# A ten-stage transformer kernel: q, k and v as rows with a late row scale, attention products one step deep, low parts written over the raw weights

## The chip, the cores and the metric

The kernel runs on one core of one Trainium2 chip. The metric is the device time of one execution in microseconds (us), lower is better. Beside the time of each run there is one profiled execution with its own time and its span, from the first to the last instruction.

## The reference, cut to what matters

256 tokens of width 1024, float32, pass ten stages; each is `x = x + c * rms_norm(f(rms_norm(x)))`.

```python
# moba:  z = h @ w_in (1024 x 2560): gated unit, 8 heads of causal attention, causal convolution; @ w_out
# cross: q = h @ w_xq; k, v = split(m @ w_xkv); 4 heads of 256; @ w_xo     (m: normed memory, 256 rows)
# relu:  square(relu(h @ w_ff1)) @ w_ff2                                  (1024 x 4096 x 1024)
# glu0..glu3: (silu(h @ wg) * (h @ wu)) @ wd                              (width 2816)
# diff:  q, k, v = split(h @ w_in, 3)                                     (1024 x 3072)
    q = concatenate([_rotate(q[..., :16], ang), q[..., 16:]], -1)    # per 64 columns; k alike
#        8 heads: softmax(q1 k1) - lam * softmax(q2 k2), times v, then a norm of each head's 128 columns
# near:  q, k, v = split(h @ w_in, 3); 16 heads of 64 with a relative bias inside a window; @ w_out
def rms_norm(x, g):
    return x * rsqrt(mean(x * x, -1) + EPS) * g
```

The order is moba, cross, relu, glu0, diff, glu1, glu2, near, glu3.

## The kernel before, in words

**Chunks.** All weights pass as 226 chunks of 1 MB, each 128 partitions x 2048 float32. SyncE loads a chunk into one of three `raw` buffers (`load`, L373); ScalarE casts it to a rounded high part (`w_hi<-raw`, L555); VectorE subtracts to get the low part (`w_lo<-raw,w_hi`, L772). A product takes three matmuls for each tile: high x high, high x low, low x high. Cast and subtraction of one chunk are the word `s` of the plan (or `h` and `l` apart). Load c waits for `lo_done`: the subtraction of chunk c-3, which frees its raw buffer (L376). The high and low parts have three slots of their own, and a fourth that lies over `qT`/`kT` in the stages that do not hold them (`slots_of_chunks`). A cast waits until the chunk that held its slot has been used.

**The plan.** `PLAN` is a table of words for each stage; every engine walks the same words in order and does its part of each. `q1` is a chunk's product, `.0` and `.1` its halves (for in-rows products the two tiles of 128 tokens), `:0`/`:1` halves by tokens of a product that lies transposed. `post`, `gain`, `sq`, `turn` are steps of the norm between stages for token tile 0 or 1: scale and add the result, multiply the gain, squares, and the turn of the rows by TensorE to `hT`.

**Products.** `transposed` (L1086) holds a 128 x 128 weight tile and moves 256 tokens, giving q or k with heads on the partitions; `in_rows` (L1101) holds a token tile and moves up to 512 weight columns. Before, q and k are `transposed` in all four attention stages, and v of diff and near is `in_rows`. Cross has three q chunks in the `:` form, in which every weight tile is used twice with 128 tokens each. diff multiplies each q and k by a matrix (`rot`, L1244) and mixes with cosines and sines over 128 x 512 elements (L1036, L1038, L1040).

**The row scale.** The norm's 1/root is put in at the turn for the attention stages: `diagonal` (L795) makes a diagonal matrix from it, which waits for squares (ScalarE) and root (GpSimd), and the turn is a matmul with that (L1127, 16 half steps). For the FFN stages the turn is a transpose by the identity (L1125, 8), and the scale comes in at the activation (`LATE_SCALE`, L73).

**Attention steps.** In step s, TensorE makes the scores of unit s (S, L1146 or L1141), turns the probabilities of unit s-1 (P, L1157) and weighs the values of unit s-2 (W, L1172 or L1185). A half or a whole chunk stands between two steps. VectorE finds the maximum (M, L961) and normalises (N, L969 to L981), ScalarE takes the exponential (E, L618) and copies the turned probabilities (Q, L628). diff adds a norm for each unit: squares (A, ScalarE L647), a root (GpSimd L517, L518), the scaling (B, VectorE L991), a turn (Z, TensorE L1193), and the copy and subtraction of the result (O, L607 and L1010). These letters are used below.

Of the kernel before, what the change touches and what calls it, by code (L numbers as in the profile page):

```python
# [14 lines left out]
P = 128  # L15
# [5 lines left out]
NRAW = 3  # L21
# [11 lines left out]

HEAD_GLU = ("ga0.0 post1 s gb0.0 gain1 s ua0.0 turn1 sq1 ub0.0 G0.0 H0.0 ga0.1 s gb0.1 G0.1 s ua0.1 s "
# [5 lines left out]
             "ub1.1 G1.0 H1.0 G1.1 H1.1 s da0 s db0 s ")  # L40
# [3 lines left out]
HEAD_V = "va0.0 post1 s vb0.0 gain1 sq1 s vc0.0 turn1 vd0.0 va0.1 "  # L44
PLAN = {
# [22 lines left out]
CHUNK_NAMES = {"moba": "g a u w K V q k v o", "cross": "q o", "relu": "ua ub da db",  # L68
               "diff": "va vb vc vd q k o", "near": "va vb vc vd q k o"}
GLU_NAMES = "ga gb ua ub da db g u d"  # L70
N_NORMS = len(STAGES)

LATE_SCALE = {i + 1 for i, kind in enumerate(STAGES) if kind in FFN}  # L73

Word = namedtuple("Word", "name digit form half c n first done step_next at")


def read_plans():

    plans, chunks, c_next = {}, [], 0  # L80
    for at, kind in enumerate(STAGES):
        names = CHUNK_NAMES.get(kind, GLU_NAMES).split()
        seen, n_next, words = {}, 0, []
        for text in PLAN[kind].split():
            form = ":" if ":" in text else "." if "." in text else ""
            text, half = (text[:-2], int(text[-1])) if form else (text, None)
            name = text.rstrip("0123456789")
# [11 lines left out]
            words.append(Word(name, digit, form, half, c, n, first, done, False, at))
        real = [i for i, w in enumerate(words) if w.name not in "shl"]  # L100
        for i, after in zip(real, real[1:]):
            words[i] = words[i]._replace(step_next=words[after].name == "step")
        plans[kind] = words
# [10 lines left out]
def slots_of_chunks():  # L114


    held, slots, before = [-1] * 4, [], []
    for c, (kind, name, _) in enumerate(CHUNKS):
        free = range(4) if kind in FFN or name in ("va", "vb", "vc", "vd") else range(3)
        slot = min(free, key=lambda s: held[s])  # L120
        slots.append(slot)
        before.append(held[slot])
        held[slot] = c
    return slots, before


SLOT, BEFORE = slots_of_chunks()


ATT = {  # L130
    "moba": dict(units=8, u0=0, e0=0, per_out=2, scale=0.125, parts=1, per_chunk=4),
    "cross": dict(units=4, u0=8, e0=4, per_out=1, scale=1.0 / 16, parts=1, per_chunk=1),
    "diff": dict(units=8, u0=12, e0=8, per_out=1, scale=0.125, parts=2, per_chunk=2),
    "near": dict(units=16, u0=20, e0=16, per_out=2, scale=0.125, parts=1, per_chunk=4),
}
# [11 lines left out]
def products_of(kind, s):

    a = ATT[kind]
    number = {(w.name, w.digit): w.n for w in WORDS[kind] if w.c is not None}  # L150
    heads = []
    if s < a["units"]:
        heads += [(letter, s // a["per_chunk"]) for letter in "qk"]
    if s >= 2:
        heads.append(("v", (s - 2) // a["per_chunk"]))
    return N0[kind] + 1 + max(number.get(head, 0) for head in heads)


ROT_ORDER = [w.digit for w in WORDS["diff"] if w.name == "rot"]
# [6 lines left out]
def shape_tables():  # L166
# [9 lines left out]
    mean = np.full((P, P), 1 / P, np.float32)  # L176
    rot = np.zeros((P, P), np.float32)
    inv = np.float32(500000.0) ** (-np.arange(0, 16, 2, dtype=np.float32) / np.float32(16))
    ang = (t.astype(np.float32)[:, None] * inv[None, :].astype(np.float32)).astype(np.float32)
# [1252 lines left out]
```

## Time and profile before

| | us |
|---|---|
| median of 3 runs | 1533.74 (1533.03 to 1534.62) |
| profiled execution, its time | 1531.81 |
| its span | 1530.1 |

| engine | busy, share of the span |
|---|---|
| TensorE matmul (PE) | 95% |
| TensorE weight load (PEld) | 80% |
| VectorE (DVE) | 56% |
| ScalarE (ACT) | 45% |
| GpSimd (POOL) | 9% |

The profile lists for each engine its busy time, the waits and what ended them, and the chain that ended last. A matmul's own duration overlaps its neighbour's, so the pace of TensorE is read from starts or from counts in a window.

### The profile page before, as it was taken

What the parts mean: (1) busy time and instruction counts of PE and PEld (TensorE: products, weight loads), DVE (VectorE), ACT (ScalarE), POOL (GpSimd) and SP (SyncE); (2) the same over time, 40 slices, a digit from 0 to 9 for tenths busy, and PEclk for the clock granted to TensorE, in tenths of its full rate; (3) what the DMA queues carried; (4) which work ended last, traced back from release to release, by engine and by line L of the source; (5) the groups of instructions that cost most, each with busy time, mean ns of one, the idle gap of its engine ahead of it and who ended that gap; (6) DMA issues with size and microseconds to landing.
All of it is one profiled execution on the core that took longest, in us unless ns stands there. A gap on an engine that the chain in (4) does not pass through costs nothing.

```text
span 1530.1 us, 18751 instructions
## 1 busy us (share of the span) xinstructions
PE 1454.7 (95%) x7753; PEld 1231.5 (80%) x7753; DVE 851.8 (56%) x910; ACT 689.2 (45%) x886; POOL 139.7 (9%) x248
## 2 busy tenths in 40 slices
PE   6999899999999999998679999999999899999996
PEld 6998798788888888887558888888888777688885
DVE  4976635555475445646656454655446565655443
ACT  4546435444445444444345444444334444454441
POOL 1000100101101110000011111011100600000000
PEclk9999999999999999999899999999999999999998
DMA  8754233656547655452226555476554623265550
GB/s 273 242 168 136 91 121 120 233 190 198 190 159 240 195 189 188 150 173 83 83 83 225 192 195 192 153 239 196 190 195 138 202 73 108 90 228 192 192 165 28
DMA packets 133664, 256.28 MB, mean 167 GB/s; under 512 B 6280, under 2 KB 57164, under 8 KB 133580
## 3 DMA queue, kind: packets, MB, share of 16 engines
q1 hardware_dynamic: 129484, 251.94, 49.9%
q0 software_dynamic: 4096, 3.15, 0.7%
q8 instruction: 61, 1.00, 0.3%
q14 instruction: 23, 0.19, 0.0%
HBM read 254.02 MB, written 1.05 MB: 167 GB/s over the span
## 4 chain that ended last, share of the span: by engine, by line
PE 89%; DVE 3%; ACT 3%; issue 2%; DMA 1%; POOL 1%; SPq 1%; DVEq 0%; POOLq 0%; ACTq 0%
PE ps L1108 23%; PE ps L1110 23%; PE ps L1109 23%; PE ps L1094 4%; PE ps L1096 4%; PE ps L1095 4%; PE ps L1146 2%; PE ps L1185 2%; PE ps L1334 2%; PE ps L1157 1%; DVE w_lo L772 1%; ACT w_hi L555 1%; ACT t L618 1%; DMA raw<-w_in 1%; PE ps L1125 1%
## 5 line engine op out<-in xcount | busy, mean ns | idle before, releaser
L772 DVE TENSOR_TENSOR w_lo<-raw,w_hi 128x2048 fp32r<-128x2048 f32 x226 | 519.4, 2300 | 446.3 <-ACT w_hi L555 446.0
L555 ACT CAST w_hi<-raw 128x2048 fp32r<-128x2048 f32 x226 | 431.1, 1910 | 398.8 <-PE ps L1110 368.0
L1108 PE MATMUL ps<-w_hi,hT_hi 128*128 128x512 f32 (+1 forms) x1008 | 377.7, 375 | 1.9 <-DVE w_lo L772 1.6
L1110 PE MATMUL ps<-w_hi,hT_lo 128*128 128x512 f32 (+1 forms) x1008 | 374.0, 371 | 0.0
L1109 PE MATMUL ps<-w_lo,hT_hi 128*128 128x512 f32 (+1 forms) x1008 | 373.6, 371 | 0.0
L1108 PE MATMUL ps<-w_hi,yT_hi 128*128 128x512 f32 (+1 forms) x672 | 261.5, 389 | 14.4 <-DVE rope_t L1036 7.5
L1109 PE MATMUL ps<-w_lo,yT_hi 128*128 128x512 f32 (+1 forms) x672 | 257.8, 384 | 0.0
L1110 PE MATMUL ps<-w_hi,yT_lo 128*128 128x512 f32 (+1 forms) x672 | 257.4, 383 | 0.0
L1108 PEld LDWEIGHTS ps<-w_hi,hT_hi 128*128 128x128 f32 x1008 | 189.9, 188 | 37.4 <-DVE w_lo L772 5.2
L1110 PEld LDWEIGHTS ps<-w_hi,hT_lo 128*128 128x128 f32 x1008 | 189.9, 188 | 32.9
L1109 PEld LDWEIGHTS ps<-w_lo,hT_hi 128*128 128x128 f32 x1008 | 190.0, 189 | 31.6
L1108 PEld LDWEIGHTS ps<-w_hi,yT_hi 128*128 128x128 f32 x672 | 128.3, 191 | 43.2 <-DVE w_lo L772 14.8
L1110 PEld LDWEIGHTS ps<-w_hi,yT_lo 128*128 128x128 f32 x672 | 128.1, 191 | 24.9
L1109 PEld LDWEIGHTS ps<-w_lo,yT_hi 128*128 128x128 f32 x672 | 128.1, 191 | 23.2
L1094 PE MATMUL ps<-hT_hi,w_hi 128*128 128x256 f32 (+1 forms) x480 | 140.7, 293 | 4.1 <-DVE hT_lo L801 2.7
L1095 PE MATMUL ps<-hT_lo,w_hi 128*128 128x256 f32 (+1 forms) x480 | 136.0, 283 | 0.0
L1096 PE MATMUL ps<-hT_hi,w_lo 128*128 128x256 f32 (+1 forms) x480 | 135.8, 283 | 0.0
L475 POOL DMA_DIRECT2D big<-na_rpb x128 | 66.2, 519 | 498.6 <-PE ps L1110 498.3
L1094 PEld LDWEIGHTS ps<-hT_hi,w_hi 128*128 128x128 f32 x480 | 93.1, 194 | 10.2 <-issue 8.2
L1095 PEld LDWEIGHTS ps<-hT_lo,w_hi 128*128 128x128 f32 x480 | 93.1, 194 | 0.8 <-issue 0.5
L1096 PEld LDWEIGHTS ps<-hT_hi,w_lo 128*128 128x128 f32 x480 | 93.0, 194 | 0.0
L487 POOL TENSOR_SCALAR rstd<-ssq 128x1 f32<-128x1 f32 x38 | 14.7, 388 | 714.8 <-ACT probT L561 696.3
(151 smaller groups left out, 1138.7 us busy)
## 6 DMA issues: line engine op xcount, KB each, us to landing
raw<-ffn_wg SPq DMA_DIRECT2D x44, 1024.0 KB, 5.3
raw<-ffn_wu SPq DMA_DIRECT2D x44, 1024.0 KB, 5.3
raw<-ffn_wd SPq DMA_DIRECT2D x44, 1024.0 KB, 5.3
raw<-w_ff SPq DMA_DIRECT2D x32, 1024.0 KB, 5.6
raw<-diff_w_in SPq DMA_DIRECT2D x12, 1024.0 KB, 5.1
raw<-na_w_in SPq DMA_DIRECT2D x12, 1024.0 KB, 5.1
raw<-w_in SPq DMA_DIRECT2D x10, 1024.0 KB, 5.6
raw<-w_xkv SPq DMA_DIRECT2D x8, 1024.0 KB, 5.8
```

The source lines that it names most:

```text
L475: pool.dma_start(bias[p:p + 1], bass.AP(rpb.tensor, (5 - r) * 31 + 15 - c, [[465, 16], [31, 6], [1, 64]])).then_inc(bias_in, 16)
L555: act.copy(hi_part(c), raw[:, c % NRAW, :]).then_inc(hi_done, 1)
L772: dve.tensor_tensor(lo_part(c), raw[:, c % NRAW, :], hi_part(c), ALU.subtract).then_inc(lo_done, 1)
L1094: pe.matmul(o, hi, src[0][:, k, tokens], start=(k == 0), stop=False)
L1095: pe.matmul(o, hi, src[1][:, k, tokens], start=False, stop=False)
L1096: ins = pe.matmul(o, lo, src[0][:, k, tokens], start=False, stop=(k == KT - 1))
L1108: pe.matmul(o, hi, wh[:, i, cols], start=first and i == 0, stop=False)
L1109: pe.matmul(o, hi, wl[:, i, cols], start=False, stop=False)
L1110: ins = pe.matmul(o, lo, wh[:, i, cols], start=False, stop=last and i == len(tiles) - 1)
L1146: ins = pe.matmul(o, qT[rows, head // 2, t * P:(t + 1) * P], kT[rows, head // 2, :], start=True, stop=True)
L1185: ins = pe.matmul(o, values[:, kt, cols], probT[:, b, 256 * kt:256 * kt + 256], start=(kt == 0), stop=(kt == TT - 1))
L1334: ins = pe.transpose(up_bank(kind, b, t)[:, cols], hraw[:, t, cols], ident)
```

## The change

1. q, k and v of cross, diff and near all come `in_rows`, as groups of 512 columns: chunks `qa qb` (two halves of the 1024 inner rows) are group q0, `qc qd` q1, and so on. ScalarE copies a group's rows out of PSUM times the row scale (`rq`, `rk`, `rv`); TensorE turns q and k (`tq`, `tk`); ScalarE copies the turned tile. The rotation of diff touches 16 of each 64 columns of the rows, four small VectorE operations for a tile.
2. The turn of the norm is a transpose for all stages but the first; no diagonal matrix for cross, diff and near. `lambda` moves from diff to relu.
3. The steps are written by `attention`: S of unit s, then the step's chunks, then P of s-1 and W of s-2; a split follows one step after its chunk. moba, cross, diff and near use it.
4. `raw` has five buffers, and the low part is written over the raw chunk. There are four high slots, at all times. Load c waits for `chunk_used` of c-5.

```diff
-NRAW = 3
+NRAW = 5
+NHI = 4
+def attention(kind, units, fill, carry=0):
+    lags = 4 if kind == "diff" else 3
+    words = []
+    for s in range(units + lags - 1):
+        def unit(names, lag):
+            words.extend(f"{name}{s - lag}" for name in names if 0 <= s - lag < units)
+        if kind == "diff":
+            unit("B", 3)
+        unit("SM", 0)
+        if kind == "diff":
+            unit("ZO", 3)
+        unit("E", 0)
+        chunks = fill.get(s, "").split()
+        words += chunks
+        unit("N", 0)
+        words += ["s"] * carry
+        carry = sum(word[0] in "qkvo" and not word.endswith(".0") for word in chunks)
+        unit("PQ", 1)
+        unit("WA" if kind == "diff" else "WO", 2)
+    return " ".join(words + ["s"] * carry) + " "
-HEAD_V = "va0.0 post1 s vb0.0 gain1 sq1 s vc0.0 turn1 vd0.0 va0.1 "
+HEAD_QK = ("qa0.0 post1 s qb0.0 gain1 s ka0.0 turn1 rq0.0 kb0.0 tq0.0 sq1 rk0.0 qa0.1 s qb0.1 tk0.0 s rq0.1 ka0.1 s "
+           "tq0.1 kb0.1 s rk0.1 va0.0 tk0.1 ")
-    "cross": ("q0:0 post1 s gain1 sq1 q1:0 turn1 q2:0 q0:1 s q1:1 h 0 l q2:1 h 1 l q3.0 2 q3.1 h 3 l "
-              "o0.0 o0.1 s 4 s o1.0 5 o2.0 o3.0 post0 gain0 o1.1 s o2.1 turn0 sq0 o3.1"),
+    "cross": ("qa0.0 post1 s qb0.0 gain1 s qc0.0 turn1 rq0.0 sq1 qd0.0 tq0.0 qa0.1 s rq1.0 qb0.1 tq1.0 s rq0.1 qc0.1 "
+              "s tq0.1 " +
+              attention("cross", 4, {0: "qd0.1 rq1.1", 1: "tq1.1", 3: "o0.0", 4: "o0.1", 5: "o1.0"}) +
+              "o2.0 o3.0 post0 gain0 o1.1 s o2.1 turn0 sq0 o3.1"),
+    "diff": (HEAD_QK +
+             attention("diff", 8, {0: "va0.1 vb0 rv0", 1: "qc0 qd0.0", 2: "qd0.1 rq1 kc0", 3: "tq1 kd0 rk1 vc0.0 tk1",
+                                   4: "vc0.1", 5: "vd0.0", 6: "vd0.1 rv1", 7: "o0.0", 8: "o0.1", 9: "o1.0",
+                                   10: "o2.0 o1.1"}) +
+             "o3.0 post0 gain0 o2.1 turn0 sq0 o3.1"),
...
+        w_lo = nc.alloc_sbuf_tensor_at("w_lo", [P, NRAW, CH], F32R, offset=nc.sbuf_base - 4 * NRAW * CH)
+        w_hi = sb("w_hi", [P, NHI, CH], F32R)
...
                 if c >= NRAW:
-                    sp.wait_ge(lo_done, c - NRAW + 1)
+                    sp.wait_ge(used, c - NRAW + 1)
...
-                if BEFORE[c] >= 0:
-                    act.wait_ge(used, BEFORE[c] + 1)
+                if c >= NHI:
+                    act.wait_ge(used, c - NHI + 1)
...
+            def rows_word(kind, word):
+                letter, nb = word.name[1], word.digit
+                g, count = group_at(kind, letter, nb)
+                for t in range(TT) if word.half is None else (word.half,):
+                    bank = group_bank(g, t)
+                    k = TT * (word.at + 1) + t
+                    if word.name[0] == "t":
+                        act.wait_ge(rows_turned[t], count)
+                        dst = qT if letter == "q" else kT
+                        act.copy(dst[:, 4 * nb:4 * nb + 4, t * P:(t + 1) * P],
+                                 bank.rearrange("p (k s) -> p k s", k=4)).then_inc(qk_evac[t], 1)
+                        continue
...
+                        act.activation(rows[:, t, :], bank, ACT.Copy, scale=rstd[:, k:k + 1]).then_inc(rows_out[t], 1)
```

**Where instructions move.** The unit's norm in diff, TensorE. A step of the kernel before, from the turn of unit s-3 to the next product:

```order
L1193 MATMUL ps<-tab,sub_out 128x128 [waits sub_on,b_evac]
L1193 MATMUL ps<-tab,sub_out 128x128
L1146 MATMUL ps<-kT,qT 128x256 [waits exp_ready,rope_done]
L1146 MATMUL ps<-kT,qT 128x256 x3
L1157 MATMUL ps<-tab,prob 128x128 [waits probT_ready,prob_ready]
L1157 MATMUL ps<-tab,prob 128x128 x3
L1172 MATMUL ps<-vv,probT 128x128 [waits out_lo,probT_ready]
L1172 MATMUL ps<-vv,probT 128x128 x3
L1094 MATMUL ps<-hT_hi,w_hi 128x256 [waits b_evac,lo_done]
```

The same place after the change, from the last turn of group k1 (reading `rows`) to the next product:

```order
L1308 MATMUL ps<-tab,rows 128x128 [waits rope_done_1]
L1308 MATMUL ps<-tab,rows 128x128 x3
L1160 MATMUL ps<-tab,prob 128x128 [waits probT_ready,prob_ready]
L1160 MATMUL ps<-tab,prob 128x128 x3
L1175 MATMUL ps<-vv,probT 128x128 [waits probT_ready,out_lo,v_evac_1,v_evac_0]
L1175 MATMUL ps<-vv,probT 128x128 x3
L1149 MATMUL ps<-kT,qT 128x256 [waits exp_ready,qk_evac_1,qk_evac_0]
L1149 MATMUL ps<-kT,qT 128x256 x3
L1196 MATMUL ps<-tab,sub_out 128x128 [waits sub_on]
L1196 MATMUL ps<-tab,sub_out 128x128
L1110 MATMUL ps<-w_hi,hT_hi 128x512 [waits qk_evac_1]
```

Before, a half chunk stood between W (`probT`,`vv`) and the turn Z (`sub_out`) of the same unit, and Z opened the step. Now S (`kT`,`qT`) alone stands between them, and the product comes behind Z.

ScalarE at the end of that same step (step 3 of diff) after the change; `rows<-ps,rstd` is the scaled copy of group k1, `kT<-ps` the copy of its turned tiles:

```order
L724 ACTIVATE rows<-ps,rstd 128x512 [waits rows_turned_0,r_pre,chunk_half_used]
L724 ACTIVATE rows<-ps,rstd 128x512 [waits rows_turned_1,r_pre,chunk_used]
L713 COPY kT<-ps 128x4x128 [waits rows_turned_0]
L713 COPY kT<-ps 128x4x128 [waits rows_turned_1]
L561 CAST w_hi<-raw 128x2048 [waits chunk_used,chunk_landed_1]
L561 CAST w_hi<-raw 128x2048 [waits chunk_used,chunk_landed_2]
L628 COPY probT<-ps 128x512 [waits out_ready,probT_turned]
L636 ACTIVATE att_bias,sub_stat<-ps 128x128 [waits sub_sq,out_ready]
```

Both casts of the step stand behind the copies of the turned tiles and ahead of Q (`probT<-ps`) and A (`sub_stat<-ps`), on which the next Z hangs. Before, the cast of a step stood behind A:

```order
L607 CAST yT_hi<-ps 128x256 [waits sub_turned]
L618 ACTIVATE t,denom<-ps,neg_top 128x256 [waits prob_ready,max_ready]
L618 ACTIVATE t,denom<-ps,neg_top 128x256 x3
L628 COPY probT<-ps 128x512 [waits out_ready,probT_turned]
L647 ACTIVATE att_bias,sub_stat<-ps 128x128 [waits sub_sq,sub_on,out_ready]
L647 ACTIVATE att_bias,sub_stat<-ps 128x128 [waits sub_sq]
L699 COPY kT<-ps 128x512 [waits chunk_used]
L555 CAST w_hi<-raw 128x2048 [waits chunk_used,chunk_landed_1]
```

ScalarE in the head of diff after the change, from the cast of its fifth chunk to the second copy of token tile 1:

```order
L561 CAST w_hi<-raw 128x2048 [waits chunk_used,chunk_landed_4]
L713 COPY kT<-ps 128x4x128 [waits rows_turned_0]
L561 CAST w_hi<-raw 128x2048 [waits chunk_used,chunk_landed_0]
L724 ACTIVATE rows<-ps,rstd 128x512 [waits rows_turned_1,r_pre,chunk_used]
L561 CAST w_hi<-raw 128x2048 [waits chunk_used,chunk_landed_1]
L713 COPY qT<-ps 128x4x128 [waits rows_turned_1]
L561 CAST w_hi<-raw 128x2048 [waits chunk_used,chunk_landed_2]
L724 ACTIVATE rows<-ps,rstd 128x512 [waits rows_turned_1,r_pre,chunk_used]
L713 COPY kT<-ps 128x4x128 [waits rows_turned_1]
```

The scaled copies of tile 1 (`rows_turned_1`) stand behind casts, each of which waits for a chunk to land.

## Rows read from the trace of the kernel before

**Rows 1.** The page: the chain that ended last, by engine.

```profile
PE 89%; DVE 3%; ACT 3%; issue 2%; DMA 1%; POOL 1%; SPq 1%; DVEq 0%; POOLq 0%; ACTq 0%
```

**Rows 2.** Windows: busy time, clock, DMA of stages cross, diff, near (columns: first line).

```profile
core 0: us, PE busy (x) PEld busy (x) DVE busy (x) ACT busy (x) POOL busy (x), PEclk, DMA share, GB/s
...
183.20:262.40 79.20, 78.39 (x537) 72.11 (x536) 37.55 (x49) 32.54 (x56) 4.96 (x8) 1.00 0.33 111
...
636.50:802.20 165.70, 134.57 (x810) 116.17 (x809) 96.33 (x152) 72.51 (x162) 12.71 (x24) 0.93 0.34 114
...
1178.50:1330.90 152.40, 141.78 (x794) 112.53 (x792) 89.27 (x154) 72.28 (x137) 26.81 (x24) 0.98 0.36 117
```

**Rows 3.** Windows inside three product runs; the first (x) counts matmuls.

```profile
183.20:193.80 10.60, 10.60 (x97) 10.58 (x95) 6.04 (x8) 3.88 (x7) 3.74 (x4) 1.00 0.41 151
...
310.90:321.70 10.80, 10.80 (x49) 8.97 (x48) 5.34 (x3) 4.40 (x3) 1.03 (x2) 1.00 0.54 192
...
1232.50:1235.50 3.00, 3.00 (x25) 2.92 (x24) 1.77 (x5) 1.57 (x5) 0.00 (x0) 1.00 0.00 0
```

**Rows 4.** Waits of PE, whole span: us in total, times, longest.

```profile
PE ps L1127 <- DVE rope_t L795: 13.6, 4, 10.3
...
PE ps L1108 <- DVE rope_t L1036: 7.5, 1, 7.5
...
PE ps L1146 <- issue: 5.8, 1, 5.8
```

**Rows 5.** Timeline of PE, two turns: start us, us, engine, line, out<-in.

```profile
193.88 2.00 PE L1127 MATMUL ps<-rope_t,t 128*128 128x128 f32 x16
...
810.70 1.03 PE L1125 MATMUL ps<-tab,t 128*128 128x128 f32 x8
```

**Rows 6.** Timeline of DVE at the end of moba.

```profile
174.49 1.28 DVE L786 TENSOR_TENSOR t<-x_rows,gain 128x512 f32<-128x512 f32 x2
...
176.62 0.28 DVE L795 TENSOR_SCALAR rope_t<-tab,rstd 128x128 f32<-128x128 f32 x1 [0.85 <-POOL rstd L488]
```

**Rows 7.** Timeline of PE, a turn Z of diff.

```profile
767.32 0.41 PE L1193 MATMUL ps<-tab,sub_out 128*128 128x128 f32 x2 [2.62 <-DVE sub_out L991]
```

**Rows 8.** Timeline, the norm of one unit of diff, from its product to its turn.

```profile
779.09 0.48 PE L1108 MATMUL ps<-w_hi,yT_hi 128*128 128x512 f32 x1
...
780.52 0.70 POOL L518 TENSOR_TENSOR sub_stat<-sub_stat,minus_half 128x2 f32<-128x2 f32 x1
...
782.01 0.41 PE L1193 MATMUL ps<-tab,sub_out 128*128 128x128 f32 x2
```

**Rows 9.** Timeline of DVE, unit 0 of diff: maximum, normalising, next split.

```profile
685.36 1.22 DVE L961 TENSOR_REDUCE top<-ps 128x4 f32<-128x1024 f32 x1
...
690.73 2.29 DVE L772 TENSOR_TENSOR w_lo<-raw,w_hi 128x2048 fp32r<-128x2048 f32 x1
```

**Rows 10.** Windows: clock after two idle times of PE.

```profile
704.50:709.50 5.00, 4.97 (x22) 4.24 (x23) 1.40 (x2) 1.39 (x7) 0.00 (x0) 0.50 0.46 186
...
767.30:771.30 4.00, 3.98 (x23) 3.47 (x23) 1.82 (x3) 1.35 (x6) 0.00 (x0) 0.68 0.02 4
```

**Rows 11.** Timeline, head of relu.

```profile
277.68 1.91 ACT L555 CAST w_hi<-raw 128x2048 fp32r<-128x2048 f32 x1 [3.06 <-PE ps L1110]
...
284.95 1.08 ACT L730 CAST yT_hi<-ps 128x512 fp32r<-128x512 f32 x2
...
288.12 0.47 PE L1108 MATMUL ps<-w_hi,yT_hi 128*128 128x512 f32 x1 [1.45 <-DVE yT_lo L1061]
```

**Rows 12.** Timeline of ACT, head of glu0.

```profile
462.89 1.91 ACT L555 CAST w_hi<-raw 128x2048 fp32r<-128x2048 f32 x1 [1.64 <-PE ps L1110]
...
477.52 1.91 ACT L555 CAST w_hi<-raw 128x2048 fp32r<-128x2048 f32 x1 [3.24 <-DMA raw<-ffn_wd]
```

**Rows 13.** DMA issues: count, KB each, median us to landing.

```profile
raw<-ffn_wg SPq DMA_DIRECT2D x44, 1024.0 KB, 5.3
```

**Rows 14.** Window: DMA while two loads were queued.

```profile
271.00:276.00 5.00, 5.00 (x28) 4.23 (x27) 2.59 (x4) 2.89 (x7) 0.86 (x2) 1.00 1.02 407
```

More of the change, by code:

```diff
@@ L67 @@
 FFN = ("relu", "glu0", "glu1", "glu2", "glu3")
-CHUNK_NAMES = {"moba": "g a u w K V q k v o", "cross": "q o", "relu": "ua ub da db",
-               "diff": "va vb vc vd q k o", "near": "va vb vc vd q k o"}
-GLU_NAMES = "ga gb ua ub da db g u d"
+IN_ROWS = [letter + part for letter in "qkv" for part in "abcd"]
+CHUNK_NAMES = {"moba": "g a u w K V q k v o".split(), "relu": "ua ub da db".split(),
+               "cross": IN_ROWS + ["o"], "diff": IN_ROWS + ["o"], "near": IN_ROWS + ["o"]}
+GLU_NAMES = "ga gb ua ub da db g u d".split()
 N_NORMS = len(STAGES)
-LATE_SCALE = {i + 1 for i, kind in enumerate(STAGES) if kind in FFN}
-Word = namedtuple("Word", "name digit form half c n first done step_next at")
+Word = namedtuple("Word", "name digit half c n first done at")
 def read_plans():
@@ L96, in read_plans @@
                     c_next += 1
-                    n_next += kind not in FFN and name != "o" and name[1:] == ""
+                    n_next += kind == "moba" and name != "o"
                 c, n = seen[name, digit]
[L99 to L102, printed above, removed]
+            words.append(Word(name, digit, half, c, n, first, done, at))
         plans[kind] = words
@@ L111 @@
 FIRST = [min(c for c, key in enumerate(CHUNKS) if key[0] == kind) for kind in STAGES]
[L114 to L127, printed above, removed]
 ATT = {
[L131 to L134, printed above, removed]
-}
@@ L147, in products_of @@
[L147 to L159, printed above, removed]
+GROUPS = {kind: [(w.name[0], "abcd".index(w.name[1]) // 2) for w in WORDS[kind] if w.first and w.name[1:] in ("a", "c")]
+          for kind in ("cross", "diff", "near")}
@@ L160, with number_of, group_at @@
+QK0 = {"cross": 0, "diff": 2, "near": 6}
+VV0 = {"diff": 0, "near": 2}
+def number_of(letter, digit):
+    return [w.n for w in WORDS["moba"] if (w.name, w.digit) == (letter, digit)][0]
+def group_at(kind, letter, nb):
+    g = GROUPS[kind].index((letter, nb))
+    same = [i for i, other in enumerate(GROUPS[kind][:g + 1]) if (other[0] == "v") == (letter == "v")]
+    return g, (VV0 if letter == "v" else QK0)[kind] + len(same)
 OUT_ORDER = {kind: [w.digit for w in WORDS[kind] if w.name == "o" and w.first] for kind in ATT}
@@ L513, in _ @@
                         pre_root(n, t)
[L514 to L515 removed]
+                    if kind == "diff" and word.name == "B":
+                        u = word.digit
                         pool.wait_ge(sub_sq_done, TT * (u + 1))
@@ L527, in _ @@
                                 load_bias(bias_rows[kind] + p)
-                    if kind == "near" and (word.name, word.digit, word.first) == ("q", 0, True):
+                    if kind == "near" and word.name == "rk" and (word.digit, word.half) == (0, 0):
                         pool.wait_ge(bias_in, 16 * P)
@@ L831, in norm_word @@
                     gain_rows(n, x, t)
-                if word.name == "sq" and n not in LATE_SCALE:
-                    diagonal(n, t)
                 if word.name == "turn":
@@ L1116, in turn @@
                     pe.wait_ge(h_lo, 4 * n + 2)
-                late = n in LATE_SCALE
-                if not late:
-                    pe.wait_ge(diag_set, len([m for m in range(n) if m not in LATE_SCALE]) * TT + t + 1)
+                if n < 2:
+                    pe.wait_ge(diag_set, TT * n + t + 1)
                 for b in range(2):
```

414 lines of the change are left out of this document (197 added, 217 removed), and 9 rows, old and new, of the table PLAN.

## The prediction

> **What bounds the kernel now.** I read the page first: TensorE is 89% of the chain that ended last [rows 1]. The reader should see that only TensorE's own work, its pace or its idle time can move the end. The windows by stage say where idle time is [rows 2]: cross lasts 79.2 us, diff 165.7, near 152.4, of which TensorE is idle for 0.8, 31.1 (165.7 less 134.57) and 10.6. The clock in diff is 0.93 on average, which loses 0.07 x 165.7 = 11.6 us more; in near 0.98, 3.0 us. The FFN stages have almost none of either. Third, the windows inside product runs give the pace [rows 3]: 48 matmuls of 512 columns in 10.8 us, 5.4 us a chunk; q or k with 256 columns, 25 in 3.0 us, 0.12 each, 5.76 us a chunk of 48; the `:` form of cross, 97 in 10.6 us, 0.109 each, and a chunk needs 96 of them, 10.5 us. Fourth, TensorE's waits [rows 4]: it waits for the diagonal matrix (13.6 us in four places), and in diff for the rotation (7.5, and the 5.8 put down to issue, which ends when the rotation of k1 ends).
>
> **The change, part by part.** The sum is made against the profiled execution, 1531.8 us.
>
> *Turns of the norm.* A turn by the diagonal takes 2.00 us by its row, by the identity 1.03 [rows 5]: 1.0 less. At the end of moba the gain's first half is ready at 174.49 + 0.64 = 175.1, the diagonal at 176.9 [rows 6], so turn0 starts 1.8 earlier. With one W instead of two behind the last step of moba (0.6), moba gives -3.3. The same turns at the ends of glu0 and glu2 had next to no wait: -1.1 each, -2.2.
>
> *Cross.* Three chunks leave the `:` form: 3 x (10.5 - 5.4) = 15.3 less, and turn1 1.0 less. Four turned groups of four transposes cost half a turn each, 0.5: +2.0. New waits come in the head. A load now waits for the use of chunk c-5, and the head uses the first halves of four chunks before it finishes the first. Count from the end of qa0.1: the sixth chunk's load starts there and lands 5.3 us later [rows 13]; its cast takes 1.9 [rows 12], to 7.3. Only then can ScalarE copy the rows of tile 1 (0.6, a copy is half of a pair of 1.08 [rows 11]), to 7.9, where TensorE has been since 6.2: 1.8 of wait. A gain of 0.5 MB and the seventh chunk follow; at 407 GB/s [rows 14] they take 1.3 and 2.6, so that it lands at 9.3, its cast ends at 11.2, the copy of the turned tile at 11.8, and S of unit 0 starts there in place of 8.4: 3.4 of wait. In step 2, S waits for the copy of `tq1`, which stands behind E on ScalarE: 2.2, and P 0.9. With a slow clock behind the longer wait (1.3, below) and the 0.8 of idle time before set off: -15.3 - 1.0 + 2.0 + 8.3 + 1.3 - 0.8 = -5.5; I take -5.0, for the breaks between runs.
>
> *Relu.* The table of relu has hardly changed, but its loads have. The head's `T0` copies stand on ScalarE behind the cast of the seventh chunk. Before, they ran at 284.95 and the product that needs them began at 288.12 after a wait of 1.45 [rows 11]. The first chunk is used up at 277.7 [rows 11] and the second a half chunk later, at 280.4; the seventh chunk's load now waits for that, and queues behind the sixth and a gain: landed 287.0, cast to 288.9, copy and subtraction to 291.8. That is 3.7 later, and with 5.2 us of idle time the clock falls: +2.8. Relu +6.5.
>
> *glu0 to glu3.* There the fifth cast of the head already waited 3.24 us for its chunk, at 477.5, 14.6 us after the end of ga0.1 at 462.9, on which the first of these casts waited [rows 12]. By the same count it now comes at 15.6 to 15.8, and `H0.1` behind the cast before it costs 0.6. +1 each, +4. In the steady blocks a load issued as one chunk ends lands 5.3 us later, as the next ends (5.4): no cost, but no reserve for a later landing.
>
> *diff.* Work: 134.57 busy less 11.6 of slow clock is 123.0. Eight chunks at 5.4 in place of 5.76 (-2.9), turn1 (-1.0), eight group turns for sixteen rotation matmuls of about the same time (0), and some ten fewer breaks of 0.2 (a half chunk between steps takes 2.92, 779.09 to 782.01 [rows 8], in place of 2.7): 117.2. Waits: `tq0.1` stands behind the sixth chunk's cast, then VectorE's subtraction (2.3 [rows 9]) and the rotation (1.0): 10.7 on the clock of cross in place of 6.1, 4.6. S of unit 0 0.8, the turns of the norm 0.3 and 1.1 at both ends. The main one is Z. From the end of W to Z there lies A, root and B: 779.09 to 782.01, 2.9 us, which a half chunk covered exactly [rows 8]. Now S alone (1.07) stands there: 1.8 of wait for unit 0. In later steps a second ring binds. VectorE does B, M, N and a split in order, and E lies between: M starts at 685.36 and the split after N at 690.73 [rows 9], 5.4; with the split 2.3 and B 0.6, 8.3 us a step, against 5.7 us of TensorE's work in a step with a half chunk. That is about 2.7 for each of steps 5 to 7; steps 8 to 10, which have no S or a cast ahead of Q, 3.8, 2.6 and 2.6. In step 3 two casts stand ahead of Q and A: 1.2 + 3.8 + 0.6 + 0.8, root 1.0, B 0.6 make Z start 8.4 after `tk1`, where TensorE is at 2.4: 6.0. All waits: 4.6 + 0.8 + 1.4 + 1.8 + 6.0 + 8.1 + 9.0 = 31.7. Clock: after 5.8 of idle time it was 0.50 for 5 us, after 2.62 (before the Z of [rows 7]) 0.68 for 4 us [rows 10], 2.5 and 1.3 lost. Two long waits and six short ones are 12.8, less 2.6 that hides in the VectorE ring: 10.2. Together 117.2 + 31.7 + 10.2 = 159.1 against 165.7: -6.6. The gain from the rotation is thus mostly given back at Z.
>
> *near.* Idle and slow clock fall from 10.6 + 3.0 to the head's 1.9 + 0.3 + 0.8 and 1.1 twice at the end, 5.2, and 0.4 of clock: -8.0. Eight group turns +4.0, the pace of eight chunks -2.6, turn1 -1.0: -7.6. Scaled copies and turned copies are new on ScalarE, which is busy for under half of near, so they hide outside the head.
>
> Sum: -3.3 - 2.2 - 5.0 + 6.5 + 4.0 - 6.6 - 7.6 = -14.2, 1517.6 us for the profiled execution. The median of the runs shown is 1.9 above it: **1519.5 us**.
>
> *Bounds.* A rotation on 16 columns and a scaled copy out of PSUM have no row; 0.5 to 2.1 us (the three of 0.69 before) for the first moves diff by -1 to +2. A landing may take 4.7 to 7.7 us in place of 5.3. Lower end: heads of FFN free (-10.5) and the slow clock of diff away (-10): 1499. Upper end: each head 2.4 later, below: 1541.
>
> A published figure speaks against the heads: the Trainium skill, "DMA: Bandwidth & Descriptors", section "Bandwidth", gives 6.15 us for 1 MB and 341 GB/s. By that the first late load of each of eight heads would come about 0.85 us later, an estimate of 7 us more in all. The trace has 5.3 and 407 GB/s, and I go by it.
>
> **The rivals.**
>
> *Slower: the loads bind.* The raw buffer is now held until its chunk is used, two to three chunks longer. If two queued loads and a gain land at 7.7 us, as the slowest of relu's head did, in place of 5.3, every head is 2.4 later. Eight heads are 19 us, and 2 of clock: 1541. It decides from about 1.4 us a head on. For it: casts already waited for landings in the head of glu0 [rows 12]. Against it: a rate of 407 GB/s in a burst [rows 14].
>
> *The FFN heads hide it.* TensorE's order in relu and glu has slack I did not see; the 10.5 fall away and some of cross with them: 1507.
>
> *Half way to the first.* Heads 1.5 later: 1534, no change that can be told.
>
> *Transposes don't keep the clock up.* After turns of eight transposes the next matmuls ran at full pace [rows 5], and idle times under 2.3 us had no slow stretch behind them. If transposes beside a short wait leave the clock to fall, the five waits of 1.8 to 2.2 us with a turn beside them cost 1.3 each: 1526. The Trainium skill, "TensorE: Matmul & The Clock Gate", section "Part 4: PE-mode transpose", says that transposes do not count as busy work.
>
> *The words do less than they say.* The listing of instructions shows q, k and v in rows in three stages, so this has no chance of its own.
>
> **How the numbers follow.** Forecast 0.45, FFN heads free 0.22, transposes 0.08 (all faster), half way 0.08 (same), loads bind 0.17 (slower). 0.2% of the time, 3.1 us, is about what a measurement can tell. Faster 0.75, same 0.08, slower 0.17. The range runs from the lower bound to just under the worst case: 1499 to 1540.
>
> **What would show it.** In the profile after: matmuls of 256 columns in moba alone; no wait for L795 but two at the start; diff at about 159 us with a wait of some 6 us once and 2 to 3 us several times before the turn of `sub_out`; near at 145, cross at 74; ScalarE waiting for raw chunks in every head, and about 5 us of idle TensorE in relu's. I am wrong if diff is near 125 (the ring at Z does not bind), if the steady FFN blocks show idle TensorE, or if relu is as before.

## The result, and the profile after

The changed kernel takes 1557.99 us (median of 4 runs, 1553.16 to 1558.08) against 1533.38 (1532.09 to 1534.62) in the same comparison: a ratio of 1.0153, interval 1.0132 to 1.0174. It is 25 us slower. The forecast was 1519.5, faster with 0.75; the result lies above its range. The profiled executions, 1558.02 and 1531.8, differ by 26.2.

From the page after, the busy line and the chain that ended last:

```profile
PE 1446.3 (93%) x7129; PEld 1197.7 (77%) x7129; DVE 842.2 (54%) x912; ACT 700.1 (45%) x906; POOL 139.9 (9%) x248
...
PE 81%; DMA 5%; ACT 5%; DVE 4%; issue 3%; POOL 1%; SPq 0%; DVEq 0%; POOLq 0%; ACTq 0%
```

TensorE's share of the chain fell from 89% [rows 1] to 81%. DMA grew from 1% to 5%, ACT and DVE together from 6% to 9%: the end now depends on landings and on what the two other engines do with them.

The windows of cross, diff and near after (columns as in [rows 2]):

```profile
187.38:261.84 74.46, 66.05 (x305) 53.85 (x304) 37.71 (x49) 35.11 (x60) 3.38 (x9) 0.98 0.35 121
650.32:813.92 163.60, 129.54 (x609) 103.53 (x608) 86.90 (x153) 77.95 (x169) 15.00 (x25) 0.91 0.33 112
1201.75:1353.42 151.67, 140.78 (x625) 103.33 (x624) 90.44 (x153) 76.96 (x145) 27.38 (x25) 0.98 0.36 121
```

TensorE's longest waits after, in place of [rows 4]:

```profile
PE ps L1196 <- DVE sub_out L1002: 23.8, 8, 6.2
PE ps L1339 <- DVE prob L1055: 13.2, 4, 3.9
...
PE ps L1110 <- DVE yT_lo L1063: 9.3, 3, 8.8
```

In the FFN stages `ga`, `gb`, `ua`, `ub` are chunks of the first matrices and `da`, `db` of the last one. `G` (ScalarE) and `H` (VectorE) are the two halves of the activation; `T0` is the turn of the first block of hidden rows by TensorE, with the copy (ScalarE) and subtraction (VectorE) behind it, and `da0` is the first product that uses it.

The first row is Z in diff, expected. The second is `T0` of the four glu stages waiting for `H0.1`, the third nearly all relu's `da0` waiting for the low parts of `T0`: FFN stages, whose heads the change left as they were (only `lambda` is new behind relu's `da0`, and `sq0` moved at the ends of glu0 and glu2).

Where the time went is seen by stage; there are nine, not ten. A stage is counted from its first product to the next one's, moba from the start of the span and glu3 to the end of its last product, in each kernel's profiled execution (us; the experiments of below are in the table too):

| kernel | moba | cross | relu | glu0 | diff | glu1 | glu2 | near | glu3 |
|---|---|---|---|---|---|---|---|---|---|
| before | 183.2 | 79.3 | 185.2 | 188.7 | 165.7 | 187.6 | 188.7 | 152.4 | 186.6 |
| changed | 187.4 | 74.5 | 195.0 | 193.5 | 163.6 | 194.2 | 193.6 | 151.7 | 190.3 |
| e1_before_ring5 | 181.6 | 79.4 | 196.6 | 195.8 | 168.6 | 194.1 | 195.1 | 152.3 | 187.8 |
| e2_ring6 | 185.2 | 69.8 | 188.4 | 189.0 | 161.2 | 189.0 | 188.6 | 148.3 | 186.6 |
| e3_heads | 187.5 | 74.4 | 185.6 | 189.0 | 163.7 | 188.9 | 189.1 | 152.1 | 186.6 |
| e4_z_late | 190.1 | 75.1 | 194.1 | 193.2 | 157.7 | 193.8 | 193.9 | 152.7 | 188.5 |
| e5_cast_first | 179.9 | 73.4 | 194.7 | 193.6 | 164.6 | 193.6 | 193.3 | 146.9 | 190.4 |
| e6_ring6_heads | 185.3 | 71.5 | 183.6 | 187.4 | 161.0 | 187.3 | 187.3 | 148.3 | 186.6 |
| e7_ring6_heads_cast | 177.8 | 70.1 | 183.5 | 187.3 | 161.4 | 187.3 | 187.3 | 143.0 | 186.6 |
| e8_all | 177.9 | 68.3 | 183.6 | 187.3 | 155.0 | 187.3 | 187.4 | 144.5 | 186.6 |
| e9_before_heads | 183.2 | 79.4 | 183.5 | 188.7 | 165.7 | 187.3 | 188.6 | 150.7 | 186.6 |
| e10_before_ring5_heads | 183.3 | 79.4 | 185.4 | 190.2 | 168.4 | 189.1 | 190.4 | 152.0 | 186.6 |
| e11_heads_cast | 179.2 | 72.9 | 184.8 | 188.6 | 165.5 | 188.9 | 189.6 | 145.2 | 186.6 |
| e12_bias_later | 189.9 | 75.1 | 192.7 | 188.5 | 164.5 | 188.9 | 188.6 | 151.5 | 190.3 |
| e13_gains_later | 185.4 | 74.9 | 192.9 | 190.1 | 161.9 | 190.2 | 190.2 | 150.5 | 186.6 |

Five FFN stages lose 29.8 us together (936.8 to 966.6) and moba 4.2; cross, diff and near gain 4.8, 2.1 and 0.7. That is +26.4, the whole difference. moba's own spread must be kept in mind: it is 185.2 to 190.1 in seven kernels with the same order of moba. The granted clock goes with it: its mean over moba is 0.96 in the two at 190 (e4, e12) and 0.98 or 0.99 in the five at 185 to 188. The rows are of one execution each, and that isn't always a middling one: it lies 6.3 us above the median of its kernel in e4, 6.0 above in e12, 3.5 above in e1 and 4.1 below in e13.

**The head of relu.** ScalarE after, to be read beside [rows 11]:

```profile
277.00 1.91 ACT L561 CAST w_hi<-raw 128x2048 fp32r<-128x2048 f32 x1 [3.09 <-PE ps L1112]
281.91 1.90 ACT L561 CAST w_hi<-raw 128x2048 fp32r<-128x2048 f32 x1 [1.56 <-DMA raw<-w_ff]
289.76 1.90 ACT L561 CAST w_hi<-raw 128x2048 fp32r<-128x2048 f32 x1 [5.95 <-DMA raw<-w_ff]
291.56 1.06 ACT L746 CAST yT_hi<-ps 128x512 fp32r<-128x512 f32 x2
```

and TensorE, which needs those copies:

```profile
294.73 0.76 PE L1110 MATMUL ps<-w_hi,yT_hi 128*128 128x512 f32 x1 [8.77 <-DVE yT_lo L1063]
```

The third cast (seventh chunk) begins 12.8 us behind the first, before it was 5.45 (277.68 to 283.13). It is this cast that the copies of `T0`, long turned, stand behind. The 49 matmuls that follow run for 13.38 us at a granted clock of 0.81, where 48 took 10.97 at 1.00 before.

### The profile page after: what moved, and what is told of

It is laid out like the page before. It is cut to its first block, busy times and chain, and to the rows that moved or that the text cites. A ratio compares the mean times of both kernels' runs of the same rounds, so it can differ in the third digit from the quotient of the medians.

```text
span 1556.2 us, 17556 instructions
## 1 busy us (share of the span) xinstructions
PE 1446.3 (93%) x7129; PEld 1197.7 (77%) x7129; DVE 842.2 (54%) x912; ACT 700.1 (45%) x906; POOL 139.9 (9%) x248
## 4 chain that ended last, share of the span: by engine, by line
PE 81%; DMA 5%; ACT 5%; DVE 4%; issue 3%; POOL 1%; SPq 0%; DVEq 0%; POOLq 0%; ACTq 0%
PE ps L1110 24%; PE ps L1112 23%; PE ps L1111 23%; ACT w_hi L561 3%; DMA raw<-ffn_wd 2%; PE ps L1339 2%; PE ps L1098 1%; PE ps L1100 1%; PE ps L1099 1%; DMA raw<-ffn_wu 1%; PE ps L1188 1%; PE ps L1149 1%; PE ps L1129 1%; DVE w_lo L788 1%; ACT t L620 1%
## 5 line engine op out<-in xcount | busy, mean ns | idle before, releaser
L1110 PE MATMUL ps<-w_hi,hT_hi 128*128 128x512 f32 (+1 forms) x1168 | 448.9, 384 | 0.9 <-DVE yT_lo L1063 0.5
L1111 PE MATMUL ps<-w_lo,hT_hi 128*128 128x512 f32 (+1 forms) x1168 | 441.3, 378 | 0.0
L1112 PE MATMUL ps<-w_hi,hT_lo 128*128 128x512 f32 (+1 forms) x1168 | 441.1, 378 | 0.0
L1110 PEld LDWEIGHTS ps<-w_hi,hT_hi 128*128 128x128 f32 x1168 | 223.8, 192 | 48.6 <-issue 6.1
L1112 PEld LDWEIGHTS ps<-w_hi,hT_lo 128*128 128x128 f32 x1168 | 222.9, 191 | 40.6
L1111 PEld LDWEIGHTS ps<-w_lo,hT_hi 128*128 128x128 f32 x1168 | 223.5, 191 | 37.9
L740 ACT ACTIVATE att_bias<-ps,rstd 128x512 f32<-128x512 f32 (+1 forms) x64 | 42.4, 665 | 63.4 <-PE ps L1112 63.3
L1055 DVE SCALAR_TENSOR_TENSOR prob<-ps,rstd,att_bias 128x512 f32<-128x512 f32 (+1 forms) x64 | 45.1, 713 | 20.6 <-PE ps L1112 11.2
L827 DVE SCALAR_TENSOR_TENSOR t<-ps,gain 128x512 f32<-128x512 f32 x36 | 24.6, 690 | 41.3 <-ACT probT L567 41.3
L1339 PE MATMUL ps<-tab,prob 128*128 128x128 f32 x240 | 33.2, 278 | 13.2 <-DVE prob L1055 13.2
```

Source lines behind the costliest of these rows:

```text
L740: act.activation(gate[:, t, 0:width], src[:, 0:width], ACT.Relu if kind == "relu" else ACT.Silu, scale=rstd[:, k:k + 1]).then_inc(gate_don ...
L827: dve.scalar_tensor_tensor(t1[:, t, half_row], ps[:, 2 * t + b, :], half.get(j, 1.0), gain[:, 0, half_row], ALU.mult, ALU.mult).then_inc(y ...
L1055: dve.scalar_tensor_tensor(hraw[:, t, 0:width], up_bank(kind, b, t)[:, 0:width], rstd[:, k:k + 1], gate[:, t, 0:width], ALU.mult, ALU.mult ...
L1110: pe.matmul(o, hi, wh[:, i, cols], start=first and i == 0, stop=False)
L1111: pe.matmul(o, hi, wl[:, i, cols], start=False, stop=False)
L1112: ins = pe.matmul(o, lo, wh[:, i, cols], start=False, stop=last and i == len(tiles) - 1)
```

## Experiments

Theory L: the loads are let go late, because the low part lies over the raw chunk, and this costs the FFN heads. Rival O: the order of the words costs it. `used` in the code is the semaphore that the listings call `chunk_used`. For moba theory R, a ring through VectorE.

**Loads alone: e1 and e2.** e1 adds the wait of the change to the kernel before; e2 gives the changed kernel a sixth buffer.

```diff
 e1: if c >= NRAW:
         sp.wait_ge(lo_done, c - NRAW + 1)
+    if c >= 5:
+        sp.wait_ge(used, c - 4)
 e2:
-NRAW = 5
+NRAW = 6
-gated_u = sub_out[:, :, :].rearrange("p a s -> p (a s)")
+gated_u = rows[:, 0, :]
-sub_out = sb("sub_out", [P, 2, S])
+sub_out = att_bias[:, 1, :].rearrange("p (a s) -> p a s", a=2)
 ...
```

> The kernel before with one wait more: from chunk 5 on, the load of chunk c also waits until chunk c-5 is used, which is the wait that the changed kernel has instead of its own. Nothing else moves. Theory L (late loads: the FFN heads lose because the raw buffer is held until its chunk is used): relu +9, glu0, glu1 and glu2 +5 each, glu3 +2, together 24 to 28 us over the kernel before, about 1559, with the cast of relu's seventh chunk waiting some 6 us for its landing. Rival O (order: the change loses by the order of its words and by the steps of attention, and the loads are late without cost): within 3 us of the kernel before.

> The changed kernel with six raw buffers in place of five (sub_out and gated_u lie in other buffers to make room), so that the load of chunk c waits for the use of chunk c-6; nothing moves on the engines. Theory L: a load in a head starts one chunk, some 5 us, earlier, and all five FFN heads come back to their lengths of before: relu -9, glu0 to glu2 -5 each, glu3 -2, and 1 to 4 us in the heads of cross, diff and near; 1528 to 1533. Rival O: within 3 us of the changed kernel, 1558.

Measured: e1 1562.27, 1.0195 of the kernel before (1.0171 to 1.0219); e2 1521.34, 0.9934 (0.9913 to 0.9954). One wait more makes the kernel before as slow as the changed one, with its FFN stages at 969.4 (966.6 in the changed kernel) and the same picture in relu (wait of 9.25 before `da0`). One buffer more brings the changed kernel's back to 941.6. Theory L holds. e1's five FFN stages lost 32.6 us where 24 to 28 were expected; the cast of relu's seventh chunk waited 6.3 us. e2 gained 13 us more in cross, near, diff and moba (4.7, 3.4, 2.4, 2.2), and the whole is 7 us under the range that I had expected; moba's part is within its spread.

**Order in the FFN heads: e3.** The loads stay late; only what stands behind the waiting cast is moved ahead.

```diff
 HEAD_GLU:
-ga0.1 s gb0.1 G0.1 s ua0.1 s ub0.1 H0.1 s
+ga0.1 s gb0.1 G0.1 s ua0.1 ub0.1 H0.1 s s
 the first block behind it:
-ga1 s T0 gb1
+ga1 T0 s gb1
 HEAD_RELU:
-ub0.1 G0.1 H0.1 s ua1.1 s T0
+ub0.1 G0.1 H0.1 s ua1.1 T0 s
```

> The changed kernel with its five raw buffers, but in the head of each FFN stage T0 stands ahead of the split before it, and in the glu heads H0.1 stands ahead of the split before it too; TensorE's own order is the same. If the late landing costs only because the copies and subtractions of the hidden rows stand behind the waiting cast on ScalarE and VectorE, the wait in front of da0 in relu (8.8) and of T0 in the glu stages (3.6 to 3.9) falls to 1 to 2 us: 13 to 18 us less, about 1543. If TensorE waits for the late chunk itself, the idle time only moves behind T0, to the chunk whose cast was put off: within 4 us of the changed kernel.

Measured: 1530.31, 0.9989 (0.9978 to 1.0); 28 less than the changed kernel where 13 to 18 were expected, and FFN stages of 939.2 together. ScalarE in the head of relu:

```profile
276.96 1.91 ACT L561 CAST w_hi<-raw 128x2048 fp32r<-128x2048 f32 x1 [3.06 <-PE ps L1112]
282.38 1.91 ACT L561 CAST w_hi<-raw 128x2048 fp32r<-128x2048 f32 x1 [2.07 <-DMA raw<-w_ff]
284.19 1.06 ACT L746 CAST yT_hi<-ps 128x512 fp32r<-128x512 f32 x2
290.00 1.91 ACT L561 CAST w_hi<-raw 128x2048 fp32r<-128x2048 f32 x1 [4.75 <-DMA raw<-w_ff]
```

The seventh chunk is cast at 290.00, as late as ever (13.0 behind the first), and TensorE waits 1.41 instead of 8.77. So theory L is true only with half of O: the late landing costs little itself (7 us over five stages, by e6 and e10 below). It costs most because copies that TensorE needs sooner stand behind the waiting cast on an engine that works in order.

**Z in diff: e4.** Z and O of unit s-3 behind the chunk.

```diff
-        if kind == "diff":
-            unit("ZO", 3)
         unit("E", 0)
         chunks = fill.get(s, "").split()
         words += chunks
+        if kind == "diff":
+            unit("ZO", 3)
```

> The changed kernel, with Z and O of unit s-3 in diff behind the chunk of the step instead of ahead of it, so that the chunk again lies between W and Z. If the chain W, A, root, B, Z alone makes the eight waits before Z (23.8 us together), most of them go and diff falls by 12 to 18 us, clock included, to 146 to 151. If the work of ScalarE and VectorE in a step (casts ahead of Q and A, the split behind N) is the bound, as the prediction had it for steps 5 to 7, the idle time comes back before P or W and diff gains 3 to 6 us.

Measured: 1547.01, 1.0104 (1.0077 to 1.013); diff 157.7, 5.9 less. The waits before Z fall from 23.8 to 4.6, and 11.1 appear before W, for the low part of O. The second expectation was right: the rings through ScalarE and VectorE hold back most of the gain in diff. The median fell by 11 us; the stages of the one profiled execution show 4.7 of them.

**Cast and E: e5.** In the steps of attention:

```diff
+        words += ["h"] * carry
         unit("E", 0)
 ...
         unit("N", 0)
-        words += ["s"] * carry
+        words += ["l"] * carry
```

> The changed kernel with ScalarE's cast of a step's split ahead of E of that step, where the kernel before had it, and VectorE's subtraction behind N as it is. Theory R (the ring M, E, N, subtraction sets the length of a step of moba, because VectorE waits 0.9 to 1.5 us behind N for a cast that begins only after E): the ring falls from 7.1 us to about 6.0, the waits of TensorE in moba (0.62 + 1.56, 0.84 + 1.55 and the 1.32 put down to issue) go for the most part, and moba falls from 187.4 to 182 to 184; diff falls by 2 to 6 in steps 4 to 7, near by up to 1. The stages of FFN stay. 1545 to 1552 in all. Rival: moba's 4 us are the two steps that have no chunk in them (6 and 8), whatever stands where on the other engines; moba stays at 186 to 190 and the whole within 3 us of the changed kernel.

Measured: 1544.57, 1.0086 (1.0059 to 1.0113), 13 less than the changed kernel; moba 179.9 and near 146.9, more than expected, diff 164.6, nothing where 2 to 6 were expected. VectorE in moba, in the changed kernel:

```profile
137.82 0.17 DVE L973 TENSOR_SCALAR neg_top<-top 128x2 f32<-128x2 f32 x1
...
141.42 2.29 DVE L788 TENSOR_TENSOR w_lo<-raw,w_hi 128x2048 fp32r<-128x2048 f32 x1 [1.46 <-ACT w_hi L561]
...
145.07 0.17 DVE L973 TENSOR_SCALAR neg_top<-top 128x2 f32<-128x2 f32 x1
```

and in e5_cast_first:

```profile
139.89 0.17 DVE L974 TENSOR_SCALAR neg_top<-top 128x2 f32<-128x2 f32 x1
...
141.95 2.29 DVE L789 TENSOR_TENSOR w_lo<-raw,w_hi 128x2048 fp32r<-128x2048 f32 x1
...
145.93 0.17 DVE L974 TENSOR_SCALAR neg_top<-top 128x2 f32<-128x2 f32 x1
```

From the end of one maximum to the end of the next: 7.25 us with the cast behind E, 6.04 with it ahead (6.06 in the kernel before, whose steps had it ahead). The pair shown of e5 is one step further on than the other; the step that matches lasts 6.04 in e5 too. A step that TensorE fills with S, P, W and half a chunk lasts 5.5. Behind the long ring TensorE had waits of 0.6 to 1.6 in moba, and behind the pair at 159.4 and 161.6 the clock was at its lower level, 0.50, for 3.4 us. Steps 6 and 8 have no chunk in e5 either, with waits of 0.3 and 0.4 there, and moba is shorter than in the kernel before: the rival falls.

**Together: e6, e7, e8.** The edits of e2 and e3; with that of e5; with that of e4.

> Six raw buffers and the order of e3_heads together. If both take away the same idle time in the FFN heads (the late landing costs only through what stands behind its cast), they don't add up: the FFN stages are those of e3_heads (185.6, 189.0, 188.9, 189.1, 186.6), relu 3 less than with six buffers alone, and the attention stages those of six buffers alone (69.8, 161.2, 148.3): 1516 to 1520. If they add up (two different losses), the FFN heads fall another 3 us each below the kernel before: about 1505.

> e6_ring6_heads with the cast ahead of E too. By theory R another 4 to 8 us less than e6_ring6_heads, in moba and diff; by its rival no difference over 2 us.

> e7_ring6_heads_cast with Z and O behind the chunk in diff. e4_z_late took 5.9 us from diff and left 11.1 us of waits before W for VectorE's subtraction of O; with the cast ahead of E, VectorE comes to them sooner. If the ring of VectorE and ScalarE is what is left, diff falls to 147 to 153 and the whole is 1500 to 1508; if the casts only change places with E, diff stays at 156 to 158 and the whole is 5 us under e7_ring6_heads_cast or less.

Measured: 1512.26 (0.9877, 0.9862 to 0.9891), 1497.81 (0.9777, 0.9763 to 0.9792) and 1492.11 (0.974, 0.9725 to 0.9754). e6: the two cures of the FFN heads are for the most part one (932.2, where each alone gave 941.6 and 939.2; added up they would have made 914), but 7 us more go than I expected. e7: 14 us more, moba 7.5 and near 5.3 of it, where 4 to 8 in moba and diff were expected; diff got nothing. e8: 5.7 us less than e7, and diff 155.0, between the two expectations. The kernel is 39 us, 2.6%, faster than the one before. The longest of its waits in total is W in diff, for the low part of O:

```profile
PE ps L1176 <- DVE yT_lo L1022: 11.1, 7, 4.4
```

**How much is the order alone: e9, e10, e11.** e9 is the kernel before with e3's order, e10 has e1's wait too; e11 is the changed kernel with the orders of e3 and e5, on its five buffers.

> The kernel before, whole, with the order of e3_heads in the FFN heads (T0 and H0.1 ahead of the split). Its casts waited little for landings, so little can be won: the 1.4 of wait in relu and what the glu heads of six buffers with this order are shorter (189.0 to 187.4), 1.4 each in four glu stages at most: 4 to 7 us less than the kernel before, 1525 to 1528. What this gives is no merit of the change, and the rest of the distance to e8_all is.

> e1_before_ring5 (30 us slower than the kernel before) with the order of e3_heads. If the late landing costs only through what stands behind the waiting cast, the 30 us go but for the attention stages (diff was 3 us longer): 1528 to 1538. If the landing itself starves TensorE here, it stays above 1550.

> The changed kernel with its five raw buffers, and only its words in another order: e3_heads and e5_cast_first together. They touch different stages, so they add: -28 and -13 of 1558, 1515 to 1519, faster than the kernel before by about 1%. If with five buffers the cast ahead of E holds E up for a landing, less than the sum: 1520 to 1530.

Measured: 1527.37 (0.9968, 0.9954 to 0.9982), 1536.26 (1.0025, 1.001 to 1.004), 1515.15 (0.989, 0.9875 to 0.9905), all as expected. The kernel before wins 5 us by the order of the FFN heads; with that order, the wait that cost it 30 us costs 9, of which 7 lie in the FFN stages (941.7 against 934.7). The changed kernel, on its own memory, is 1.1% faster than the one before once its words stand in another order. Of e8's 39 us under the kernel before, some 5 are thus no merit of the change. What more raw buffers would give the kernel before was not tried.

**What slows the landing: e12, e13.**

```diff
 e12: for p in range(32):
-        if 27 * p // 32 == i:
+        if 10 + 17 * p // 32 == i:
 e13:
-if c == FIRST[at] + 6:
+if c == FIRST[at] + (14 if kind in FFN else 6):
-if c == FIRST[at] + 7 and at < N_NORMS - 1:
+if c == FIRST[at] + (15 if kind in FFN else 7) and at < N_NORMS - 1:
```

> The changed kernel; GpSimd's loads of the bias rows for near (32 in each of relu, glu0, glu1 and glu2, of 24 KB in small pieces) start behind the eleventh chunk of the stage instead of the first. In relu the seventh chunk landed 10.1 us after its load was let go, where I had counted 7.3, at 261 GB/s in place of 407. If the small pieces of the bias take the rest of the rate, it lands 1 to 2 us earlier: relu -2 to -4, glu0, glu1 and glu2 -1 to -3 each (they become like glu3, which loads no bias and loses 3.7 instead of 5 to 6), together 5 to 12 less than 1558. If they are too few (0.1 MB of 3.5) to matter, under 3 us.

> The changed kernel; in the FFN stages the two rows of gains (0.5 MB each, spread over all partitions) are loaded ahead of the fifteenth and behind the sixteenth chunk instead of the seventh and eighth. By size they take 1.3 us each at 407 GB/s, and one of them lies ahead of the seventh chunk in relu: it lands 1.3 to 3 us earlier, relu -2 to -5, each glu head (glu3 too) -1 to -3, together 6 to 14 less than 1558. If the loads are held by their release alone (the use of the chunk five before) and not by the queue, under 3 us.

Measured: e12 1538.36 (1.0035, 1.0022 to 1.0047), e13 1541.13 (1.0053, 1.0035 to 1.007): 20 and 17 less than the changed kernel, both more than expected (5 to 12 and 6 to 14); their FFN stages are 949.0 and 950.0 together. Windows from the second to the third of these casts, in the changed kernel:

```profile
281.90:289.70 7.80, 4.06 (x22) 3.10 (x21) 2.29 (x1) 1.90 (x1) 1.02 (x2) 0.99 1.03 261
```

and in e12:

```profile
285.00:289.40 4.40, 4.11 (x23) 3.15 (x21) 2.34 (x2) 1.91 (x1) 0.00 (x0) 1.00 1.02 378
```

The last two columns are the busy share of the DMA engines and GB/s. Engines equally busy move 261 GB/s with the bias pieces among the chunks, 378 without. The first and the third cast in e12, and what TensorE waits before `da0`:

```profile
280.15 1.91 ACT L561 CAST w_hi<-raw 128x2048 fp32r<-128x2048 f32 x1 [3.09 <-PE ps L1112]
...
289.41 1.90 ACT L561 CAST w_hi<-raw 128x2048 fp32r<-128x2048 f32 x1 [2.44 <-DMA raw<-w_ff]
...
294.38 0.76 PE L1110 MATMUL ps<-w_hi,yT_hi 128*128 128x512 f32 x1 [5.27 <-DVE yT_lo L1063]
```

The third cast comes 12.8 behind the first in the changed kernel (12.4 to 13.3 in e1, e3, e4 and e5, which have the same transfers), 9.3 in e12 and 10.8 in e13. So both the pieces and the gains delay it. glu3, which loads no bias, is the same in e12 (190.3) and comes back only in e13 (186.6).

## Why the prediction was wrong

- **FFN heads** (relu +6.5, glu +1 each, -2.2 for turns: +8.3; measured +29.8). The mechanism was right, down to what stands behind which cast. The step that failed is the landing: "now waits for that, and queues behind the sixth and a gain: landed 287.0". That is 9.3 behind the first cast at 277.7; measured were 12.8. The count left out GpSimd's bias pieces, which go out in the same burst; they add 3.5 us. Without them, in e12, the rest of the count comes out too: the cast is 9.3 behind, `da0` waits 5.27 where I had 5.2 us of idle time, and the fifth cast of glu0 is 15.8 behind the first where I had 15.6 to 15.8 (20.7 in the changed kernel). In glu0 to glu2 the same 3.5 (the third cast of glu0 is 12.7 behind the first, 9.3 in e12) put `H0.1`, for which I gave 0.6, behind a late subtraction: `T0` waited 3.6 to 3.9 there, with a slow clock behind it, and 0.25 to 0.7 in e12. The pieces are 17.6 of the 29.8; the 12.2 that e12 leaves are 3.9 over my sum, 2.7 of it in glu3, which has no pieces: there the gains cost 3.7 (e13), where I had 1. I took 407 GB/s from a burst without such pieces [rows 14].
- **moba** (-3.3; measured +4.2, of which 2.5 either way is its spread). The turn went as counted: no wait for the diagonal, 1.16 for the gain. The failing step is one that I didn't take: moba's part was summed by its end alone, and the attention steps, which the change rewrote, were left at zero. There the split's cast went behind E. e5 alone is 7.5 under the changed kernel, and its 179.9 is 3.3 under the 183.2 of before, as the sum had it.
- **near** (-7.6; measured -0.7). The head waited 3.3 in three places, 3.0 expected. The step that failed is that the new copies "hide outside the head": `o0.0` waits 2.59 for the copy of `rv1`. Two waits of 1.4 in the last steps had no term either; idle time is 10.9 where I had 5.2. The same cast behind E has its part in it: in e5 the 2.59 and one of the two 1.4 are gone, and near gets back 4.8 of the 6.9 that were missing.
- **diff** (-6.6; measured -2.1). The waits before Z come out at 23.8 where I had 24.9, the longest 6.2 where I had 6.0, and `tq0.1` at 4.47 for 4.6. Too small was the term of the clock: 9% of 163.6, 14.7 us, where I had 10.2. Idle time is 34.1 for 31.7, with `tk0.1` (2.56) not foreseen, and the work came out 2.4 less.
- **cross** (-5.0; measured -4.8): waits of 1.42 and 3.61 in its head, 1.8 and 3.4 expected. Right, with some luck in the rest: the two waits of step 2 were 1.7 and 0.4 for 2.2 and 0.9, and 1.3 before an output product was not foreseen.

The part of each in the miss of 40.6 us (-14.2 forecast, +26.4 measured) is 21.5, 7.5, 6.9, 4.5 and 0.2.

Of the rivals, "the loads bind" comes nearest, and in the FFN heads alone: in relu the landing is 3.5 us later where it had 2.4 for every head, and it was to decide from 1.4. The heads of cross, diff and near, for which it had the same 2.4, waited about as forecast, and its reason, a queue of two loads and a gain, was not the whole one. I gave it 0.17 for want of a row of DMA with everything in it that the new burst would have. The Trainium skill, "DMA: Bandwidth & Descriptors", section "Bandwidth", has 341 GB/s, which the prediction set aside for the 407 of [rows 14]; the head of relu ran at 261, and the page's figure would have been nearer. "Transposes don't keep the clock up" can't explain the miss. Behind a wait of 2.06 us with a turn of eight transposes after it, the 12 matmuls of a half chunk ran at full clock (x15 counts all that touch the window):

```profile
811.07:813.92 2.85, 2.85 (x15) 2.34 (x14) 1.43 (x3) 2.67 (x8) 0.56 (x2) 1.00 0.48 184
```

Behind the first turn of rows in near, after a wait of 1.97, the clock stayed up too. But in e12 and e4, after 2.01 and 1.92 in the same place, it was 0.50 for 3.4 us, so such a wait can cost up to 1.7 us, in some executions.

What stays open: by what the small pieces slow the large ones; whether the last 11.1 us before W in diff go with another place in PSUM for Z (that wasn't tried), and how much of e2's gain in cross, diff and near is the landing alone and how much the order behind it.

## What to carry to other kernels

When a buffer is held longer, list for every transfer that starts later not only its consumer but all that stands behind the consumer on its in-order engine; moving the urgent copies ahead of the cast that waits was worth 28 us net here, as much as a sixth buffer did for those stages. When words are regrouped in a table, follow the ring of each engine through one whole step, also in stages where the change "does nothing": a cast behind E in place of ahead of it was 13 us. Take a transfer rate from a stretch that has the same mix of transfers in it as the one to be predicted.

## What was unexpected of the hardware

Small pieces on GpSimd's queue weigh far more than their bytes: in the 7.8 us window above GpSimd's queue moved 0.07 of 2.04 MB, and without it (e12) the rate was 378 in place of 261 GB/s, and the seventh chunk's cast came 3.5 us sooner. GpSimd's own packets took 5.7% of the 16 engines' time in that window, and SyncE's 97.7% for 1.96 MB, where in e12 they took 101.7% of 4.4 us for 1.66 MB: a packet of SyncE's took 132 ns in place of 92, an estimate from those shares and the 921 and 779 packets. No run shows why. And TensorE, after 8.8 us of idle time, ran the next 13.4 us at a mean clock of 0.81, 2.4 us longer than the same product before: the wait cost about a quarter more than it lasted.
